# HGRN2 scores: the four-block visits of TensorE, computed in column groups instead of over the full array

## What is computed

```python
diff = b[..., :, None, :] - b[..., None, :, :]
decay = jnp.exp(jnp.where(causal[:, :, None], diff, NEG_BIG))
scores = jnp.einsum('bhtk,bhsk,bhtsk->bhts', qc, kc, decay)
o = scores @ vc + jnp.einsum('bhtk,bhkv->bhtv', qc * jnp.exp(b), state)
...
state = (jnp.exp(b_last[..., 0, :])[..., None] * state
         + jnp.einsum('bhsk,bhsv->bhkv', kc * jnp.exp(b_last - b), vc))
```

## Time and profile before

| | |
|---|---|
| median of 3 runs | 1415.5 us (1414.96 to 1415.71) |
| span of the profiled execution | 1413.9 us (its own time isn't given apart from the three; 1.6 us under the median) |
| PE busy | 1402.5 us, 99% |
| DVE busy | 989.0 us, 70% |
| ACT busy | 664.3 us, 47% |
| POOL busy | 101.5 us, 7% |
| granted TensorE clock | 1.000 over the span, the upper of the two levels |
| L776, PE | 384 MATMULs, 70.6 us busy |
| L1927, DVE | 144 masked copies |

### The profile page before, as it was taken

How to read it: one execution, slowest core, us unless ns; L and a number is a source line. 1 busy time by engine, 2 the same in 40 slices (tenths; PEclk the granted TensorE clock), 3 DMA queues, 4 the chain that set the end, 5 groups by cost and what they waited for, 6 DMA issues and landing times.

```text
span 1413.9 us, 21998 instructions
## 1 busy us (share of the span) xinstructions
PE 1402.5 (99%) x8095; PEld 1194.9 (85%) x8095; DVE 989.0 (70%) x1730; ACT 664.3 (47%) x1115; POOL 101.5 (7%) x128
## 2 busy tenths in 40 slices
PE   9999999999999999999999999999999999999999
PEld 8888888798887888887878777899888988888878
DVE  6787788764667676666666677667556678777892
ACT  6343434353555565656565666554333433443440
POOL 2112221100000000000000000000000012122120
DMA  6322222244222222222222221413334132322211
GB/s 187 90 62 77 71 60 80 59 126 117 75 75 76 75 75 75 74 74 74 74 75 75 75 73 33 130 52 105 90 90 116 51 88 61 89 65 74 85 46 60
DMA packets 211685, 113.42 MB, mean 80 GB/s; under 512 B 3743, under 2 KB 209889, under 8 KB 211602
## 3 DMA queue, kind: packets, MB, share of 16 engines
q1 hardware_dynamic: 211202, 112.02, 27.6%
q0 software_dynamic: 400, 0.28, 0.1%
HBM read 110.18 MB, written 2.10 MB: 79 GB/s over the span
## 4 chain that ended last, share of the span: by engine, by line
PE 93%; DVE 3%; ACT 2%; issue 1%; DMA 0%; SPq 0%; ACTq 0%; DVEq 0%
PE ps L602 36%; PE ps L617 35%; PE scores L776 4%; PE scores L617 4%; PE scores L977 2%; PE ps L1008 2%; PE ps L991 2%; PE ps L957 2%; PE ps L805 1%; PE ps L631 1%; PE ps L807 1%; PE scores L794 1%; DVE op_lo L1737 1%; PE ps L816 1%; PE ps L751 0%
## 5 line engine op out<-in xcount | busy, mean ns | idle before, releaser
L617 PE MATMUL ps<-w_hi,op_hi 128*128 128x512 f32 (+1 forms) x880 | 319.9, 364 | 2.9 <-DVE op_lo L1737 1.5
L602 PE MATMUL ps<-op_hi,w_hi 128*128 128x512 f32 (+1 forms) x800 | 319.4, 399 | 0.0
L617 PE MATMUL ps<-w_lo,op_hi 128*128 128x512 f32 (+1 forms) x880 | 309.4, 352 | 0.0
L617 PE MATMUL ps<-w_hi,op_lo 128*128 128x512 f32 (+1 forms) x880 | 308.7, 351 | 0.0
L602 PE MATMUL ps<-op_lo,w_hi 128*128 128x512 f32 (+1 forms) x800 | 305.7, 382 | 0.0
L602 PE MATMUL ps<-op_hi,w_lo 128*128 128x512 f32 (+1 forms) x800 | 304.6, 381 | 0.0
L1679 DVE TENSOR_TENSOR w_lo<-raw,w_hi 128x1024 fp32r<-128x1024 f32 x200 | 239.1, 1219 | 20.4 <-ACT w_hi L1198 20.3
L1198 ACT ACTIVATE w_hi<-raw 128x1024 fp32r<-128x1024 f32 x200 | 202.7, 1051 | 37.1 <-PE ps L617 13.0
L617 PEld LDWEIGHTS ps<-w_hi,op_hi 128*128 128x128 f32 x880 | 166.6, 189 | 27.1 <-issue 6.4
L577 POOL TENSOR_TENSOR scratch<-scratch 128x256 f32<-128x256 f32 x112 | 95.0, 848 | 1266.9 <-DVE scratch L1854 951.8
L617 PEld LDWEIGHTS ps<-w_lo,op_hi 128*128 128x128 f32 x880 | 166.4, 189 | 23.1
(11 more groups left out here) (217 smaller groups left out, 1855.1 us busy)
## 6 DMA issues: line engine op xcount, KB each, us to landing
raw<-in_b_w_in SPq DMA_DIRECT2D x80, 512.0 KB, 3.8
raw<-in_a_w_in SPq DMA_DIRECT2D x64, 512.0 KB, 4.2
raw<-in_c_w_in SPq DMA_DIRECT2D x24, 512.0 KB, 4.2
raw<-in_a_w_out SPq DMA_DIRECT2D x16, 512.0 KB, 4.0
raw<-in_b_w_out SPq DMA_DIRECT2D x8, 512.0 KB, 4.0
raw<-in_c_w_out SPq DMA_DIRECT2D x8, 512.0 KB, 5.0
xt<-in_x SPq DMA_DIRECT2D x4, 512.0 KB, 6.3
y<-in_norm_w SPq DMA_DIRECT2D x3, 512.0 KB, 4.3
```

What stands on the lines that cost most here:

```text
L602: last = nc.tensor.matmul(bank, a, b, start=(k == 0 and p == 0), stop=(k == KT - 1 and p == 2))
L617: last = nc.tensor.matmul(bank, a, b, start=(k == 0 and p == 0), stop=(k == KT - 1 and p == 2))
```

## The change

In all three rounds the product is cut down to key groups, each written to its own partitions of `scores2`, which on TensorE are columns of the array.

- Rounds 0 and 1: the 128 keys of a tile are cut in two windows of 64 (`WINDOW`); each is multiplied only with the queries of its own window, 96 columns. So 8 products of 64 keys x 96 columns a visit instead of 4 of 128 x 192. `keep_quad` copies each window apart, on 64 partitions: 6 masked copies instead of 3, of half the elements.
- Round 2, whose group of four blocks of 32 is the whole tile: key block b = 0, 1, 2 (32 keys) is multiplied with query block b+1 and its far versions, 96, 64 and 32 columns. So 12 products a visit. The product then holds wanted entries alone, and `keep_quad` takes them with a plain copy on 32 partitions, without a mask. To have the versions of one query block side by side, `a_far` holds them one block earlier in this round, and a third plane, `a_farthest`, holds the version that skipped two blocks; `a_qq` grows from 4 to 6 planes of 512 columns.
- The mask table shrinks to the windows' masks of two rounds.

```diff
--- before.py
+++ after.py
@@ -47,8 +47,9 @@
 QUADS = (2, 8, 32)
 G_STEPS = 2 + len(QUADS)
 KEPT = 2 + 3 * len(QUADS)
-QUAD_MASK = 3 * P // 4 + P // 2 + P // 4
-MASKS = P + P // 2 + QUAD_MASK * len(QUADS)
+WINDOW = P // 2
+QUAD_MASK = 3 * WINDOW // 4 + WINDOW // 2 + WINDOW // 4
+MASKS = P + P // 2 + QUAD_MASK * (len(QUADS) - 1)
 
 SMALL_CONSTANTS = 10
 GELU_SCALE = 2 * (2 / np.pi) ** 0.5
@@ -115,10 +116,10 @@
     masks[:, :P] = np.eye(P, dtype=np.uint8)
     masks[:, P:P + 64] = s == 2 * np.arange(64)
     at = P + 64
-    for m in QUADS:
+    for m in QUADS[:-1]:
         for blocks, back in (((1, 2, 3), 1), ((2, 3), 2), ((3,), 3)):
-            t = np.array([h + i * m + u for h in range(0, P, 4 * m) for i in blocks for u in range(m)])
-            masks[:, at:at + len(t)] = s // m == t // m - back
+            t = np.array([h + i * m + u for h in range(0, WINDOW, 4 * m) for i in blocks for u in range(m)])
+            masks[:, at:at + len(t)] = s % WINDOW // m == t // m - back
             at += len(t)
 
     i, j = np.arange(P)[:, None], np.arange(P)[None, :]
@@ -182,9 +183,9 @@
 
         zeros, ones_row = scratch[:, 0:P], scratch[0:1, P:2 * P]
         at = 0
-        a_qq, at = carve(at, 4, S)
+        a_qq, at = carve(at, 6, S)
         a_qq = a_qq.rearrange("p (h x) s -> p h x s", h=2)
-        a_q, a_far = a_qq[:, :, 0], a_qq[:, :, 1]
+        a_q, a_far, a_farthest = a_qq[:, :, 0], a_qq[:, :, 1], a_qq[:, :, 2]
         a_k, at = carve(at, 2, S)
         a_t, at = carve(at, 2, 2 * S)
         a_v, at = carve(at, 2, S)
@@ -771,10 +772,19 @@
                         pe.wait_ge(keys_moved, h * LEVELS + 2 * r + 1)
                         pe.wait_ge(sd_done, h * KEPT + 2 + 3 * r)
                         for t in range(TT):
-                            tile = slice(t * P, (t + 1) * P)
-                            of = a_qq[:, prev, :, tile].rearrange("p x (h c) -> p x h c", c=4 * m)[:, :, :, m:]
-                            last = nc.tensor.matmul(scores2[:, t * 256:t * 256 + 192], a_k[:, prev, tile], of,
-                                                    start=True, stop=True)
+                            if r == len(QUADS) - 1:
+                                for b in range(3):
+                                    keys = slice(t * P + b * m, t * P + b * m + m)
+                                    queries = slice(t * P + (b + 1) * m, t * P + (b + 2) * m)
+                                    last = nc.tensor.matmul(scores2[b * m:b * m + m, t * 256:t * 256 + (3 - b) * m],
+                                                            a_k[:, prev, keys], a_qq[:, prev, 0:3 - b, queries],
+                                                            start=True, stop=True)
+                                continue
+                            for w in range(0, P, WINDOW):
+                                window = slice(t * P + w, t * P + w + WINDOW)
+                                of = a_qq[:, prev, 0:2, window].rearrange("p x (h c) -> p x h c", c=4 * m)[:, :, :, m:]
+                                last = nc.tensor.matmul(scores2[w:w + WINDOW, t * 256:t * 256 + 96], a_k[:, prev, window],
+                                                        of, start=True, stop=True)
                         last.then_inc(g_ready, 1)
 
                     def turn_k():
@@ -1888,7 +1898,8 @@
                         q = a_q[:, prev].rearrange("p (b u m) -> p b u m", u=4, m=m)
                         far = a_far[:, prev].rearrange("p (b u m) -> p b u m", u=4, m=m)
                         moved(2 * r + 1)
-                        nc.vector.tensor_tensor(far[:, :, 2:4], q[:, :, 2:4],
+                        to = slice(1, 3) if r == len(QUADS) - 1 else slice(2, 4)
+                        nc.vector.tensor_tensor(far[:, :, to], q[:, :, 2:4],
                                                 decay[:, :, 1:3].unsqueeze(3).to_broadcast([P, nb, 2, m]),
                                                 ALU.mult).then_inc(far_done, 1)
 
@@ -1900,7 +1911,10 @@
                         decay = a_t[:, prev, start:start + 4 * nb].rearrange("p (b u) -> p b u", u=4)
                         far = a_far[:, prev].rearrange("p (b u m) -> p b u m", u=4, m=m)
                         dve.wait_ge(far_done, h * 6 + 2 * r + 1)
-                        nc.vector.tensor_tensor(far[:, :, 1], far[:, :, 3],
+                        to, of = far[:, :, 1], far[:, :, 3]
+                        if r == len(QUADS) - 1:
+                            to, of = a_farthest[:, prev].rearrange("p (b u m) -> p b u m", u=4, m=m)[:, :, 1], far[:, :, 2]
+                        nc.vector.tensor_tensor(to, of,
                                                 decay[:, :, 1].unsqueeze(2).to_broadcast([P, nb, m]),
                                                 ALU.mult).then_inc(far_done, 1)
 
@@ -1916,16 +1930,23 @@
                     def keep_quad(r, back):
 
                         m = QUADS[r]
-                        nb = P // (4 * m)
-                        to = a_sd.rearrange("p t (b c) -> p t b c", c=4 * m)[:, :, :, back * m:]
-                        of = scores2[:].rearrange("p (t c) -> p t c", c=256)[:, :, 0:192]
-                        of = of.rearrange("p t (x b c) -> p t x b c", x=2, b=nb)
-                        of = (of[:, :, 0], of[:, :, 1, :, m:], of[:, :, 1, :, 0:m])[back - 1]
-                        at = P + 64 + QUAD_MASK * r + (0, 96, 160)[back - 1]
+                        if r == len(QUADS) - 1:
+                            keys = slice((back - 1) * m, back * m)
+                            of = scores2[:].rearrange("p (t c) -> p t c", c=256)[keys, :, 0:(4 - back) * m]
+                            nc.vector.tensor_copy(a_sd[keys, :, back * m:], of).then_inc(sd_done, 1)
+                            return
+                        nb = WINDOW // (4 * m)
+                        at = P + 64 + QUAD_MASK * r + (0, 48, 80)[back - 1]
                         wide = 4 * m - back * m
-                        mask = a_mask[:, at:at + nb * wide].rearrange("p (b c) -> p b c", b=nb)
-                        nc.vector.copy_predicated(to, mask.unsqueeze(1).to_broadcast([P, TT, nb, wide]),
-                                                  of).then_inc(sd_done, 1)
+                        for w in range(0, P, WINDOW):
+                            keys = slice(w, w + WINDOW)
+                            to = a_sd[keys, :, keys].rearrange("p t (b c) -> p t b c", c=4 * m)[:, :, :, back * m:]
+                            of = scores2[keys].rearrange("p (t c) -> p t c", c=256)[:, :, 0:96]
+                            of = of.rearrange("p t (x b c) -> p t x b c", x=2, b=nb)
+                            of = (of[:, :, 0], of[:, :, 1, :, m:], of[:, :, 1, :, 0:m])[back - 1]
+                            mask = a_mask[keys, at:at + nb * wide].rearrange("p (b c) -> p b c", b=nb)
+                            last = nc.vector.copy_predicated(to, mask.unsqueeze(1).to_broadcast([WINDOW, TT, nb, wide]), of)
+                        last.then_inc(sd_done, 1)
 
                     def carry():
```

## The result

The changed kernel takes 1417.6 us (median of 20 runs, 1415.85 to 1419.3), the kernel before in the same session 1415.5 (median of 20, 1414.7 to 1416.1): a ratio of 1.0014, with a 95% interval from 1.0008 to 1.0021. The forecast was 1401.7 and the range ended at 1410. The 14 us did not come: the kernel is 2.1 us slower, clear of the noise, and still within the 0.2% that the prediction calls no change. The profiled execution stands at 1417.5 us with a span of 1415.6.

A forecast was written before the change was run, and what follows sets the result against it. TensorE, busy 99% of the span, was taken as the bound. Saving 14.4 us there, less 0.6 us of added VectorE time, made 13.8 us, so 1401.7 us from 1415.5; range 1399 to 1410.

The forecast's parts named there:

- The visit's price: TensorE time of one `quad_scores` block: 1.30 us falling to 0.99 in rounds 0 and 1, 1.02 in round 2.
- the price of the mode: Fixed TensorE cost per block of going into and out of column groups: 0.34 us, or 0.30, read from L1008.
- So three more cost 0.2 us (nearest, since they follow each other) up to 0.6 us a visit: VectorE in rounds 0 and 1: three extra copy instructions per visit add 0.2 to 0.6 us.
- 0.2 (even 0.6) fits under: Added VectorE time stays hidden: L1903 ends 1.6 us ahead of round 1's visit, 1.1 us ahead of round 2's.
- POOL's key products ... keep their distance ... since both sides count from that end: POOL's key products wait for a visit's end and keep 0.6 us of distance to `turn_k` on TensorE.
- in round 2 ... this is no more than now: VectorE in round 2: three plain copies on 32 partitions cost no more than masked ones (288 against 339 ns).
- DVE eats part of it: Rival: at 0.6 us per visit, round 2's 1.1 us cover may go, giving 1404 to 1408 us; 7%.
- issue price: Rival on TensorE: no MATMUL issues faster than 0.055 us whatever its width, giving 1419.3 us; 6%.
- uneven groups: Rival on TensorE: round 2's three widths run one after the other, 1.64 us a visit, giving 1411.6 us; 8%.
- pairs at 0.11: Rival on TensorE: weight loads keep a pair at 0.11 us, so all visits cost 1.22, giving 1412.3 us; 7%.
- no overlap: Rival on TensorE: groups never run side by side and 0.34 us per visit comes on top, 1432 us; 2%.
- PE still at 203 of 203: Sign of a right forecast: TensorE stays busy for all 203 us in windows of the A layers.

The follow-up runs named there:

- full copies: Changed kernel's column groups on TensorE in all three rounds, but the three masked copies over 128 partitions from partition 0 as in the kernel before: 1401.6 us.
- by tiles: Kernel before, with the masked copies of rounds 0 and 1 each cut in two by pairs of tiles, all on 128 partitions from partition 0: 1415.9 us.
- round 2 alone: Changed kernel with its rounds 0 and 1 undone, so that only round 2 is changed: 1411.5 us.
- copies by windows: Kernel before, TensorE unchanged, with the masked copies of rounds 0 and 1 each cut in two windows of 64 partitions: 1425.2 us.
- upper window first: Copy on partitions 64 to 127 first in each pair: kernel before with window-cut copies, 1425.2 to 1422.0 us; changed kernel, 1417.6 to 1410.6 us.
- groups in a row: Kernel with column groups and full copies, a visit's products ordered by group instead of in turn: 1415.7 us.

## Why the prediction was wrong, point by point

- *The visit's price (1.30 to 0.99 and 1.02 us)*: right. 1.01 and 1.04, a saving of 13.4 us for the forecast 14.4; the price of the mode, taken from the block of L1008, held. With full copies the kernel is at 1401.6 us; the forecast had put the change at 1401.7. There round 2's visits cost 0.97 us, since DVE is in time for them; the saving is 14.5 us.
- *"So three more cost 0.2 us (nearest, since they follow each other) up to 0.6 us a visit"*: this is the step that failed. The stretch grew by 1.25 us, not by 0.2 to 0.6. The step costed the copies by their number and their elements, from neighbours that all started at partition 0, and for that alone it was right (by tiles: 0.19). (A slip in it changes little: at 1.2 ns an element, 128 elements are 0.15 us, so a copy has 0.05 us more than its elements, not 0.07.) That the start changes between 0 and 64 took the overlap from all six copies and the last product: 0.81 us more, about 0.12 for each of the seven. The range had no term for it, and the rows that the prediction read show no DVE instruction with another start.
- *"0.2 (even 0.6) fits under"* a cover of 1.6 and 1.1 us: the cover was rightly sized, but I looked only for the next visit. With 1.25 us that of round 2 is all but used up: L1917 ends at 143.63 and the visit begins at 143.85. And the places that suffer most are others: the decays, which slip under POOL's products, and behind them the states (0.67 to 1.09 us) and, in the last two heads, PE's waits and clock.
- *"POOL's key products ... keep their distance ... since both sides count from that end"*: true of POOL, and beside the point. What changed was the distance of DVE's decays from POOL's start. I had treated POOL as an engine that PE waits for, not as one that keeps DVE waiting. With *"in round 2 ... this is no more than now"* it stands otherwise: its plain copies are held too, yet round 2 alone kept its gain.
- *The rival "DVE eats part of it"* named the right engine, with the wrong size and place: 1404 to 1408 at 7%, from the same 0.6 us and only at round 2's visit. It had neither the held starts nor what late DVE work does to the states. The rivals on TensorE (issue price, uneven groups, pairs at 0.11, no overlap) all fell: pairs are 0.082 us apart, and round 2's three widths run side by side. No price of issue binds either: MATMULs of two groups begin within 0.01 us of each other.
- *"PE still at 203 of 203"* and *"DVE busy some 6 us more"* were named as what would show the steps right; 201.22 and 38.5 show them wrong.

## What to carry to other kernels

When a TensorE result is spread over partition groups, lay it out in PSUM so that the engine that empties it can still take it in one instruction from partition 0: here that alone is the difference between 1417.6 and 1401.6 us. Cost a copy by where it starts, compared with the last instruction that used the same memory, as well as by its size, and if pieces must start elsewhere, order them so that the last one starts where the next instruction does (3 us here in the kernel with copies by windows, up to 7 in the changed one). And when an engine with 30% idle time gets later, ask what its work will newly run into, on other engines too. The sign to look for in a profile is an instruction that the change doesn't touch and whose length has changed (the decays, 292 to 583 ns).

## What the runs showed of the hardware

- **Held instructions.** In a run of DVE instructions that start at partition 0 (kernel before, by tiles), each begins mostly 0.08 to 0.1 us before the end of the last where it waits for nothing of it; after a change of the start partition against the last use of the same memory it begins 0.01 to 0.04 us behind (by windows, changed kernel). Price here: about 0.12 us each, and nothing for an instruction that waits for the one in front anyway (upper window first).
- **DVE and POOL take turns.** The timelines of DVE and of POOL in the changed kernel, behind the visit of round 2:

```profile
144.97 1.31 DVE L1844 TENSOR_TENSOR scratch<-scratch 128x128 f32<-128x128 f32 x2
```

```profile
144.89 1.31 POOL L578 TENSOR_TENSOR scratch<-scratch 128x256 f32<-128x256 f32 x2 [3.56 <-PE scores L779]
```

  Two DVE products that alone take 0.29 and 0.23 us fill 1.31 us, exactly as long as POOL's two. Where DVE starts first, it is POOL that is long: its first product at 139.72, 0.04 us behind L1883, takes 0.89 us, and those that start ahead of DVE 0.62. The masked copies, which read PSUM, ran beside POOL at no cost that can be seen. The Trainium skill (SBUF — State Buffer, "SBUF: two separate sides") states this as a lock that whichever starts first keeps for its whole instruction, when DVE has two SBUF inputs; the trace agrees in that whichever started first kept its usual length (POOL 0.62 us, DVE 0.42) and the other became longer.
- **Column groups look ahead.** In the visit with groups in a row (140.00), a group's next MATMUL starts although three of another group, issued before it, are still to run; until then the order of issue decides. In the changed kernel each group goes on at 0.082 us per MATMUL of 96 columns, and narrower groups hide beside it. In its round 2 the last MATMUL issued begins at 144.27, before two wide ones issued ahead of it (144.36 and 144.45); POOL, which waits for the semaphore of that last one, still begins only at 144.89, when all have ended (144.69).
